# Windowed attention, TensorE's order: the scores of the pair two on between the second and third group of turnings

## What is computed

```python
# 16 heads of 64, 4 key heads (each shared by 4 query heads), blocks of 128 queries
# keys of a block: a band of 384 latent keys (|i-j| <= 128) and all 256 context keys
s = jnp.einsum('bqkgd,bskd->bkgqs', q, kp).astype(F32) * scale
if m is not None:
    s = jnp.where(m, s, -jnp.inf)
...
p = jax.nn.softmax(jnp.concatenate(logits + [sink_col], axis=-1), axis=-1)
...
term = jnp.einsum('bkgqs,bskd->bqkgd', p[..., off:off + n].astype(vp.dtype), vp)
```

## Time and profile before

| what | before |
|---|---|
| median of 3 runs | 3668.06 us (3665.86 to 3669.89) |
| profiled execution | 3672.49 us |
| its span | 3670.8 us |
| mean granted TensorE clock | 0.921 |
| TensorE busy | 3018.0 us, 82% |
| VectorE, ScalarE, GpSimd busy | 33%, 18%, 9% |
| attention stage, first to last product | 2402 to 2735 us |

### The profile page before, as it was taken

One profiled execution on the slowest core, in us unless ns is written; L12 is line 12 of the kernel. 1 busy time (PEld: TensorE's weight loads), 2 busy tenths in 40 slices (PEclk: granted clock), 3 DMA queues, 4 the chain that ended last, 5 costly groups with the idle time before them and its releaser, 6 DMA issues. The chain is left out here.

```text
span 3670.8 us, 51018 instructions
## 1 busy us (share of the span) xinstructions
PE 3018.0 (82%) x18238; PEld 1569.6 (43%) x18239; DVE 1216.2 (33%) x2215; ACT 676.9 (18%) x1522; POOL 332.2 (9%) x374
## 2 busy tenths in 40 slices
PE   3999998899949939999998549868889489789991
PEld 1555554788824423333333124445555333233330
DVE  3323322766672351111110242256643501001114
ACT  2312211111120100000000131156651000000002
POOL 0000001111210010000000212201110000000002
PEclk8999999999979959999999769989999699899995
DMA  6511101232236348679978330131110389886874
GB/s 273 157 50 57 50 26 50 88 97 80 66 138 220 143 181 355 272 307 378 369 290 352 143 116 35 45 123 42 52 31 35 155 343 398 331 369 248 353 291 166
DMA packets 153503, 667.47 MB, mean 182 GB/s; under 512 B 26480, under 2 KB 62864, under 8 KB 122624
## 3 DMA queue, kind: packets, MB, share of 16 engines
q1 hardware_dynamic: 125360, 545.54, 38.7%
q0 software_dynamic: 18496, 66.64, 4.9%
q10 hardware_dynamic: 9488, 53.09, 3.5%
HBM read 595.84 MB, written 69.39 MB: 181 GB/s over the span
## 5 line engine op out<-in xcount | busy, mean ns | idle before, releaser
L1831 PE MATMUL bank<-w,xT 128*64 x3392 | 751.5, 601 | 66.4 <-DMA w<-in_moe_w 40.8
L511 PE MATMUL bank<-aT,w 128*128 128x512 f32 (+1 forms) x1344 | 487.8, 523 | 6.7 <-DVE short L712 5.9
L1831 PEld LDWEIGHTS bank<-w,xT 128*64 128x64 f32 x3392 | 249.1, 139 | 532.6 <-issue 532.5
L1851 PE MATMUL bank<-w,hT 128*64 (+1 forms) x1696 | 380.9, 602 | 55.2 <-issue 50.0
L511 PEld LDWEIGHTS bank<-aT,w 128*128 128x128 f32 x1344 | 255.1, 191 | 227.6 <-issue 215.8
L1923 DVE TENSOR_TENSOR h<-h,bank 128x512 f32<-128x512 f32 x53 | 36.5, 688 | 785.2 <-PE bank L1831 785.2
L1851 PEld LDWEIGHTS bank<-w,hT 128*64 128x64 f32 x1696 | 122.2, 138 | 277.7 <-issue 277.7
L2136 PE MATMUL bank<-at_w_in,aT 128*128 128x512 f32 x416 | 182.3, 598 | 2.9 <-PEq L116 2.9
L2328 PE MATMUL bank<-eye,probs 128*128 128x128 f32 x640 | 99.1, 286 | 45.2 <-ACT probsT L2394 45.0
L1780 POOL DMA_INDIRECT x<-moe_x,idx_block x55 | 53.4, 970 | 841.0 <-PE bank L1807 839.3
L2136 PEld LDWEIGHTS bank<-at_w_in,aT 128*128 128x128 f32 x416 | 79.2, 192 | 99.8 <-issue 99.8
(11 more groups left out here) (336 smaller groups left out, 3919.3 us busy)
## 6 DMA issues: line engine op xcount, KB each, us to landing
w<-in_moe_w SPq DMA_DIRECT2D x180, 2048.0 KB, 13.2
ada_w<-in_ada_w SPq DMA_DIRECT2D x48, 1024.0 KB, 8.6
moe_y<-y ACTq DMA_DIRECT2D x53, 512.0 KB, 10.4
w<-in_moe_w ACTq DMA_DIRECT2D x12, 2048.0 KB, 21.5
w<-in_ab_w_in SPq DMA_DIRECT2D x28, 512.0 KB, 3.9
moe_y<-zero POOLq DMA_DIRECT2D x1, 8192.0 KB, 24.9
moe_x<-a SPq DMA_DIRECT2D x13, 512.0 KB, 2.7
at_w_in<-in_at_w_in SPq DMA_DIRECT2D x3, 2048.0 KB, 16.6
```

The lines of the kernel that those rows point to most:

```text
L511: mm = pe.matmul(k.bank[3 * s + n][:, 0:width], w[j][:, c, :], aT[:, c, at:at + width], start=(c == 0), stop=(c == KC - 1))
L1831: mm = pe.matmul(k.bank[UP[half]][u * UNIT:(u + 1) * UNIT, :], xT[:, c, u * UNIT:(u + 1) * UNIT], w13[:, r if u else ds(buf[0], 1), half, ...
L1851: mm = pe.matmul(k.bank[Y[half]][u * UNIT:(u + 1) * UNIT, :], hT[:, c, u * UNIT:(u + 1) * UNIT], w2[:, r if u else ds(buf[0], 1), at:at + ...
```

## The change

In TensorE's program `turn` takes a list of the turnings to do. In the loop over the pairs it is called twice, with the first and second turning and then with the third, and the scores of pair m + 2 are issued between the two calls, no longer ahead of both. The programs of the other engines are the same.

```diff
-        def turn(m):
-            for r in range(3):
+        def turn(m, some):
+            for r in some:
                 f = fill(m, r)
                 wait_fill(pe, f)
                 for h in ((r,) if r < 2 else R2):
@@
         scores(0)
         scores(1)
         for m in range(M):
+            turn(m, (0, 1))
             if m + 2 < M:
                 scores(m + 2)
-            turn(m)
+            turn(m, (2,))
             if m % 2:
                 output(m)
```

## The result

The changed kernel takes 3802.47 us (median of 4 runs, 3801.16 to 3810.68), the kernel before 3666.96 us (4 runs, 3664.63 to 3669.89). The ratio is 1.0374, 95% interval 1.0356 to 1.0392: 136 us slower. The forecast was 3752 with a range up to 3785, so the direction was right and the size was not. It missed 50 of 136 us.

The account below looks back on a forecast made before the run. The attention's TensorE, VectorE, ScalarE ring was taken as the bound: 10.13 us a group becomes 12.86, +81.9 for 30 groups and +2.4 for the first, +84.3 on the 3668.06 median, giving 3752 us; range 3736 to 3785.

Parts of the forecast that it names:

- What bounds the kernel: Attention stage: engines handing work over without slack set the pace, 10.13 us per group of two pairs, scores at the head.
- The ring: Attention: TensorE scores, VectorE maxima, ScalarE exponentials and copies, TensorE output; 10.13 us a group before, 12.86 forecast.
- The new order on TensorE and VectorE's copy: Attention: odd pair's second turning waits for VectorE's copy behind the maxima, so both sets of maxima stand in one chain.
- what would show it: Signs in the attention: groups about 12.9 us, two TensorE waits for L2460, about 2 and 1 to 1.5 us.
- The sum of +84.3: Attention stage: +2.73 us for each of 30 groups (+81.9), +2.4 for the first group, nothing for the last.
- I take an unchanged clock, since the waits are nearer to 1.23 than to 4.89: TensorE in the attention: clock stays at 1.00 despite waits of about 2.0 and 1.5 us; no time added.
- rival 1: Attention: clock falls once per group, output at half speed, 1.8 us a group, 3808 us; 11%, 1 for staying down.
- Rival 2: Attention: only the scores' delay of 1.18 us counts, L2460 not late; 11.31 a group, +37, 3705 us; 5%.
- Rival 3: Attention: not slower, since ScalarE's wait for turnings decides; 43 us gained, 3625; 3%, 1 more for cancelling.
- The bounds: Attention handoffs: low 12.33 us a group (68 us in all), high 13.41 (102 us); 3736 to 3770.
- the middle values: Attention handoff times chosen between low and high, from the same instruction pairs in the same order; 12.86 us a group.

## Why the prediction was right and wrong

- **What bounds the kernel**: right. The ring with the scores at its head gave 10.13, and moving the scores down by 1.18, 1.55, 2.73 or 0.6 us of ring, as worked out, gave groups of 11.31, 11.61, 12.79 and 10.72 as the shortest at full clock; moving them up shortened the group to 9.17.
- **The new order on TensorE and VectorE's copy**: right. TensorE waits for L2460 twice in a group (2.1 and 1.5 us), as said under "what would show it", and in the group shown every distance up to the odd pair's second turning is within 0.01 us. The even pair's second turning waits for L2465, 0.59 after the first.
- **The sum of +84.3**: right for what it sums, 0.08 a group too much. The stage with a clock held at 1.00 is 82.3 us longer and its median 3752.53. That is the forecast's number, but of another kernel.
- **"I take an unchanged clock, since the waits are nearer to 1.23 than to 4.89"**: the step that failed. It put the price of the clock at nothing. A row with a wait of 1.23 and no fall and a row with 4.89 and a fall were the only ends, nearness between them decided nothing, and the row between them pointed to a fall. The waits came out at the 2.0 and 1.5 us that I had worked out, and every one of the 30 groups ran in part at half clock. It cost 53.9 us of the stage, 1.8 for each of 30 groups, and 50 us of the median. That is rival 1, with 1.8 us a group and 3808 us; it had 10%. Its sign, a clock under 0.95 in the attention, came about (0.82). The range, drawn out to 3785, left it out although it was the only rival with a row in its favour.
- **Rival 1's own account** is right in kind and near in its sum in part by luck. It had one fall in each group and a slow output behind it. In the trace the half clock lies on scores, turnings or the output, or on all in turn for 10 us, and a group costs 0.5 to 3.2 us over 12.86; only the mean is 1.8.
- **Rival 2** (1.18 alone, 3705): wrong as an account of the whole change, but its 11.31 is what the even pair's half gives at full clock.
- **Rival 3** (not slower): wrong. ScalarE's wait for turnings was never on the ring; its copies of the even pair did start earlier, 0.69 us into the group in place of 2.07 (2608.26 and, before, 2557.39), and won nothing.
- **The bounds** 3736 to 3770 on the handoffs were wide: the handoffs came out within 0.1 us of the middle values. The range should have spent that width on the clock.
- The Trainium skill, page "TensorE: Matmul & The Clock Gate", section "A second HAM failure mode: psum-queue depth-cycling", tells of a kernel whose frequent short idling between groups of products made the clock fall and rise again and again. The trace of the changed kernel agrees, with waits of about 2.1 and 1.5 us in each group and a mean clock of 0.82.

## What to carry to other kernels

Where two engines hand work to each other in a ring, find the instruction at the ring's head and read what each edit does to its start; other waits, however large in the list, are slack. When a forecast puts waits of a new size into TensorE's program, price the slow spell behind them as part of the forecast, from the same trace's products at half clock. And in a program with fixed orders on two engines, look at which bank or buffer each moved instruction now stands behind: here scores behind one turning cost 0.6 us a group at full clock, behind two 2.65.

## What was not expected of the hardware

Waits of TensorE and what followed, in one stage with the same products. A longest wait of 1.23 us (1.30 in some groups), with TensorE 85% busy: clock 1.00 throughout. 1.39 us (1.50 in some): 16 of 30 groups with a slow spell with the odd pair's order alone, 15 of 30 with the first wait filled. 1.45 us (1.51 in some): 9 of 30. 1.81: 19 of 30. 3.11: all. Two in a group, of 2.1 and 1.5: all. So the longest wait alone doesn't order them. The same wait can be followed by a slow output or a fast one, as the two neighbouring groups above show; what decides between them no run here tells. One slow spell costs 1.5 to 1.8 us of a group; in the changed kernel, with its two waits, the groups lie 0.5 to 3.2 us over 12.86.

Work that nobody reads made a kernel faster: with 22 more transpositions in a group the change took 3752.53 in place of 3802.47 us.
